# First attention of a two-block kernel: VectorE takes a unit's maxima ahead of the weighing of the unit before it, and four weight splits stand behind units 1 to 4

## What is computed

```
q, k, v, qi, ki, wi = split(rms_norm(x) @ w_in)      # 16 heads of 64, 4 key/value heads
q, k, qi, ki = rope(...)
score = sum_h relu(qi_h . ki) * wi_h,  -inf where s > t
sel = top 64 of score per token
for each key head n and its 4 query heads g:
    logits = q_ng . k_n / 8 on the selected positions, -inf elsewhere
    p = softmax(logits)
    o_ng = p @ v_n
x = x + concat(o) @ w_o
```

## Time and profile before

| | us |
|---|---|
| median of 3 runs | 1130.02 |
| lowest and highest run | 1126.76, 1133.1 |
| span of the profiled execution | 1127.7 |
| TensorE busy | 1070.8 |
| VectorE busy | 784.7 |
| ScalarE busy | 648.3 |
| GpSimd busy | 219.1 |
| first scores of attention to the output linear | 83.5 to 121.9 |

### The profile page before, as it was taken

One profiled execution on the slowest core, in us unless ns is written; L12 is line 12 of the kernel. 1 busy time (PEld: TensorE's weight loads), 2 busy tenths in 40 slices (PEclk: granted clock), 3 DMA queues, 4 the chain that ended last, 5 costly groups with the idle time before them and its releaser, 6 DMA issues.

```text
span 1127.7 us, 23316 instructions
## 1 busy us (share of the span) xinstructions
PE 1070.8 (95%) x9388; PEld 969.5 (86%) x9388; DVE 784.7 (70%) x1049; ACT 648.3 (57%) x961; POOL 219.1 (19%) x169
## 2 busy tenths in 40 slices
PE   6987899999999998999899999989999999999987
PEld 5984698899889978998698899879998899998775
DVE  4597647666769889577666667776756877775674
ACT  4667457566655694325366676654444576666552
POOL 0000033334420007924023344330000000000000
PEclk8989999999999999999899999999999999999999
DMA  6423487877744630002377877747564565656500
GB/s 230 150 76 122 139 274 246 274 261 254 236 165 151 202 101 3 4 3 78 94 246 247 268 248 256 255 140 204 185 189 149 156 205 166 204 167 206 163 2 37
DMA packets 82426, 190.53 MB, mean 169 GB/s; under 512 B 5872, under 2 KB 6272, under 8 KB 82224
## 3 DMA queue, kind: packets, MB, share of 16 engines
q1 hardware_dynamic: 73184, 157.31, 43.0%
q0 software_dynamic: 7584, 27.53, 8.4%
q10 hardware_dynamic: 1584, 4.64, 1.2%
HBM read 188.40 MB, written 1.05 MB: 168 GB/s over the span
## 4 chain that ended last, share of the span: by engine, by line
PE 81%; DVE 10%; ACT 3%; issue 3%; DMA 2%; POOL 1%; ACTq 0%; DVEq 0%; POOLq 0%; SPq 0%
PE bank L2096 13%; PE bank L2097 13%; PE bank L2098 13%; PE bank L2324 5%; PE bank L2326 5%; PE bank L2325 5%; PE bank L2072 4%; PE bank L2074 4%; PE bank L2073 4%; PE bank L2527 3%; DVE w_lo L1280 1%; DMA mod_w<-in_w_mod_dram 1%; PE bank L2639 1%; ACT probs L837 1%; PE bank L2137 1%
## 5 line engine op out<-in xcount | busy, mean ns | idle before, releaser
L1280 DVE TENSOR_TENSOR w_lo<-raw,w_hi 128x1024 fp32r<-128x1024 f32 x296 | 384.6, 1319 | 228.0 <-ACT w_hi L697 227.5
L697 ACT ACTIVATE w_hi<-raw 128x1024 fp32r<-128x1024 f32 x296 | 309.8, 1055 | 275.3 <-PE bank L2098 152.2
L2096 PE MATMUL bank<-act_hi,w_hi 128*128 128x256 f32 x1392 | 393.3, 283 | 5.0 <-DVE w_lo L1280 3.5
L2097 PE MATMUL bank<-act_lo,w_hi 128*128 128x256 f32 x1392 | 391.4, 281 | 0.0
L2098 PE MATMUL bank<-act_hi,w_lo 128*128 128x256 f32 x1392 | 391.1, 281 | 0.0
L2096 PEld LDWEIGHTS bank<-act_hi,w_hi 128*128 128x128 f32 x1392 | 264.5, 190 | 8.4 <-issue 7.0
L2097 PEld LDWEIGHTS bank<-act_lo,w_hi 128*128 128x128 f32 x1392 | 263.7, 189 | 0.7
L2098 PEld LDWEIGHTS bank<-act_hi,w_lo 128*128 128x128 f32 x1392 | 264.2, 190 | 0.0
L555 POOL TENSOR_TENSOR mod_all<-mod_all,mod_w 128x1024 f32<-128x1024 f32 x42 | 106.1, 2526 | 164.4 <-ACT mod_w L909 163.6
L2324 PE MATMUL bank<-w_hi,ff_hi 128*128 128x512 f32 x256 | 100.9, 394 | 1.7 <-DVE ff_lo L1534 1.7
L2326 PE MATMUL bank<-w_hi,ff_lo 128*128 128x512 f32 x256 | 100.9, 394 | 0.0
(11 more groups left out here) (325 smaller groups left out, 1388.1 us busy)
## 6 DMA issues: line engine op xcount, KB each, us to landing
raw<-in_mlp_w_up_dram SPq DMA_DIRECT2D x64, 512.0 KB, 5.0
raw<-in_mlp_w_down_dram SPq DMA_DIRECT2D x64, 512.0 KB, 4.5
raw<-in_dil_w_in_dram SPq DMA_DIRECT2D x64, 512.0 KB, 4.1
mod_w<-in_w_mod_dram POOLq DMA_DIRECT2D x48, 512.0 KB, 4.4
raw<-in_conv_w_in_dram SPq DMA_DIRECT2D x32, 512.0 KB, 3.8
raw<-in_rwkv_w_rkv_dram SPq DMA_DIRECT2D x24, 512.0 KB, 3.9
raw<-in_dsa_w_in_dram SPq DMA_DIRECT2D x16, 512.0 KB, 4.8
raw<-in_dsa_w_o_dram SPq DMA_DIRECT2D x8, 512.0 KB, 3.7
```

What stands on the lines that cost most here:

```text
L697: act.activation(w_hi[:, slot, :], raw[:, slot, :], ACT.Copy).then_inc(hi_ready, 1)
L1280: dve.tensor_tensor(w_lo[:, slot, :], raw[:, slot, :], w_hi[:, slot, :].bitcast(F32), ALU.subtract).then_inc(lo_ready, 1)
L2096: pe.matmul(dst, w_hi[:, slot, at], hi[:, kt, :], start=begin, stop=False, skip_group_check=True)
L2097: pe.matmul(dst, w_hi[:, slot, at], lo[:, kt, :], start=False, stop=False, skip_group_check=True)
```

## The change

In VectorE's loop over the units, `maxima(u + 1)` stands ahead of `weigh(u)` instead of behind it. The splits of `dsa_out` granules 0 to 3, which stood behind units 4, 5, 6 and 7, stand behind units 1, 2, 3 and 4. The lists of the other engines are the same.

```diff
                 maxima(0)
                 maxima(1)
                 for u in range(units):
-                    weigh(u)
                     if u and u + 1 < units:
                         maxima(u + 1)
+                    weigh(u)
                     if u < 2:
                         turned_rope(6 + u, S["qT"][:, 4 + 2 * u:6 + 2 * u, :])
                     if u >= 1:
                         rest_values(u - 1)
                     copy_pT(u)
-                    if u >= KV_HEADS:
-                        split_lo(STREAM["dsa_out"], u - KV_HEADS)
+                    if 1 <= u <= KV_HEADS:
+                        split_lo(STREAM["dsa_out"], u - 1)
```

## The result

The changed kernel takes 1141.31 us (median; 1138.8 to 1148.23), the kernel before 1130.34 beside it: a ratio of 1.0098 with a 95% interval of 1.0058 to 1.0138. It is slower, as forecast, but by twice what was forecast (11.0 us instead of 5.3), and it lies outside the range of 1131 to 1140.5.

The account below looks back on a forecast made before the run. TensorE, busy 1070.8 of 1127.7 us, was taken as the bound, with chain waits in the first attention. 2.48 + 1.18 + 0.77 + 0.89 = 5.32 gave a 1133.0 us span, plus 2.3: 1135.3 us; range 1131 to 1140.5.

Parts of the forecast that it names:

- The sum of the order: First attention: the new VectorE order lengthens the periods of units 1 to 5, delaying the output linear by 5.32 us.
- +2.48: Unit 1's period: reciprocal of unit 2 at 98.38 against 95.90, 1.34 us from the order and 1.14 from the split.
- The waits moved as said: Sign: VectorE idle before the wide maxima of units 6 and 7, no longer before the reciprocals of units 1 to 6.
- The joints of VectorE instructions: VectorE in attention: neighbours overlap by 0.08 us; without the overlap, twelve joints add 1.0 us in the worst case.
- The splits are free: Rival, units 2 and 3: reciprocals wait for scores, not VectorE; 3.7 us instead of 5.3, time 1133.7; chance 0.10.
- VectorE's way: Units 2 and 3: period through turn, VectorE's copy, split and wide maxima, 4.81 us; taken as the later way.
- the 4.57 of TensorE's: Units 2 and 3: the other way, through turn, mask product, wide scores and maxima, 4.57 us.
- Passed on whole: Behind attention: whatever delays attention's end reaches the kernel's end in full, the output linear starting at 127.25 instead of 121.93.
- A further fall of TensorE's clock: Rival, attention: longer idling on TensorE brings another half-clock fall, 1.0 to 2.1 us; time 1137.0 with 1.7; chance 0.25.
- The clock given back further on: Rival, 440 to 800 us: later arrival avoids clock falls, returning up to 7.2 us; time 1128.1; chance 0.07.

Follow-up runs that it names:

- filled changed kernel: Changed kernel plus idle, unread bf16 products on TensorE where it waits in attention: 1135.37 us, 1.0028 of the kernel before.
- narrow units only: Kernel before with the maxima ahead of the weighing in units 1 to 3 only, splits as before: 1135.5 us against 1129.96, ratio 1.0041.
- the third edit: Kernel before plus idle TensorE products, late loads issued earlier, and ScalarE's copy of a turned half behind the next exponentials in wide units: 1127.62 us, ratio 0.9975.
- the five filled executions: Executions with idle TensorE products added: changed kernel (1.0028), kernel before twice (0.9968, 0.9989), kernel before with loads issued earlier (0.9942), that with the third edit (0.9975).

## Why the prediction was wrong

- **The sum of the order: right.** 5.32 was summed; 5.29 is what separates the two kernels when the clock is up in both. The first two periods were shifted against each other, since the sum took unit 2's scores from a row at half clock, and agree together (+2.48, +2.51). That fall is in the sum's base and in its result alike (39.45 and 34.13 against 38.94 and 33.65 with full clock), so it drops out of the difference. The waits moved as said: VectorE idles before the maxima of units 6 and 7 and no longer before the reciprocals of units 1 to 6. The joints of VectorE instructions overlap as in the earlier trace rows: full-clock periods of 5.40, 4.80, 4.81, 5.23, 5.23, summed as 5.42, 4.81, 4.81, 5.22, 5.22, leave no room for the 1.0 us that the rule of the Trainium skill, "VectorE: DVE Perf Modes", section "The DRAIN you can't avoid", would have added without its exception.
- **"The splits are free": wrong as a rival**, right in part for units 2 and 3 when the maxima stay behind. In the filled changed kernel units 2 and 3 have the 4.80 and 4.81 of VectorE's way, split included, and not the 4.57 of TensorE's. Alone, the splits lengthen unit 1 (6.10 against 4.83 and 5.03); what they cost in the whole time, 1.1 us by the sum, is within the scatter.
- **Passed on whole: right** where it can be read, 1005.8 and 1005.6 us behind attention in the first pair of executions. Over all executions that part goes from 997.5 (narrow units only) to 1011.6 us (with the third edit), which is more than the effect (below).
- **The step that failed is "A further fall of TensorE's clock".** It was put at 0.25, as one fall of 1.0 to 2.1 us, against a base in which the clock is up from unit 2 on. In both executions of the changed kernel the clock was low in three stretches, from unit 1 through 2, in unit 4 and at the end. The price of one was about right: against full clock, unit 2 grew by 1.6, unit 4 by 1.4 and 1.6, the tail by 0.9 and 1.8. The count was wrong, and so the case was: it was the rule and not a rival. The argument against it, that each hole grows by 1.2 at most and that the kernel before had holes without falls, took one execution of the kernel before as its behaviour; a second one had a fall in the tail and a longer one at the front. With the clock down the later way changed too: in unit 2 the chain of the changed kernel does not pass the split, as summed, but TensorE's turn, mask and scores at half clock.

```profile
99.78 1.09 PE bank L2270 x4
100.87 0.85 PE bank L2253 x2
101.72 2.03 PE bank L2257 x8
```

- **The clock given back further on** did not show: the part behind attention is the same in the first pair and differs by 1.3 us in the second (1006.8 changed, 1008.1 before).
- **What adds up, and what does not.** Order 5.3, clock in attention 2.8 (mean of two executions each) is 8.1 us. The medians differ by 11.0, with an interval of 6.6 to 15.6 us (1.0058 and 1.0138 of 1130.34). The output linear's own start at half clock takes longer (0.80, 0.63, 0.44 for its first products instead of 0.50, 0.39, 0.40). Its first six products took 0.5 and 1.1 us longer in the changed kernel's two executions than in the first of the kernel before, but 0.9 longer in the second of the kernel before too, so this adds some 0.3 by the means. The rest, some 2.6 us, is within the interval; whether it is more falls in executions without a profile or scatter is open.

## What to carry to other kernels

An instruction that is moved ahead on an in-order engine brings its own wait with it: ask what it waits for at its new place, and who waits for what now stands behind it. Here the maxima were off the path in the wide units and the weighing on it, so the exchange could only lose. Where TensorE works in short pieces, price a longer hole not only by its length but by the clock that every piece behind it may run at, and read that from more than one execution; idle products in the holes measure that price and won most of it back here, though two of the five filled executions still had a fall.

## What the runs showed of the hardware

The place of a clock fall differs between executions of one and the same kernel: the kernel before needed 34.13 us for attention in one and 37.28 in another, 0.3% of the whole. A hole of 3.9 us with 0.63 us of work in it went before a fall, but so did the tail's pieces, where TensorE waited 1.00 and 1.62 between pieces of 1.1. The first execution had the same two waits, 1.00 and 1.63, and no fall there (period 4.03 instead of 5.80), so the holes alone do not say where a fall comes. Outside attention the stretch from the final norm of the second feed-forward to the convolution's first sum (as many products in all kernels) took from 116.1 to 127.3 us in the executions looked at; the longest ran at a granted clock of 0.93, but 116.1 and 119.5 both have 1.00, so the clock is not all of that, and its cause was not looked for. Windows of three executions (narrow units only, the changed kernel, the version with the third edit):

```profile
752.20:868.30 116.10, 113.05 (x912) 109.06 (x912) 82.86 (x113) 56.66 (x73) 4.75 (x7) 1.00 0.59 181
```
```profile
754.80:874.30 119.50, 116.45 (x912) 112.44 (x912) 82.87 (x113) 56.67 (x73) 4.75 (x7) 1.00 0.60 176
```
```profile
741.20:868.50 127.30, 124.25 (x912) 120.20 (x912) 82.95 (x112) 56.75 (x73) 4.75 (x7) 0.93 0.54 165
```
